# Sample attention of a two-layer decoder: the next batch's scores move between this batch's products

## The chip, the cores and the metric

The kernel runs on one core of a Trainium2 chip. The metric is the device time of one execution in microseconds (us). TensorE (PE) multiplies, VectorE (DVE) and ScalarE (ACT) work on what it leaves in PSUM, SyncE (SP) issues the loads from HBM.

## The reference, cut to what matters

Two layers are computed for 512 prompt tokens and for 8 sample batches of 4 tokens; the change lies in the native sparse attention (NSA) of the sample batches alone. Each batch has 4096 past positions in pages of 128, chosen by a page table.

```python
s_c = einsum('btkgd,bckd->bkgtc', qg, kc)            # compressed branch: 128 block means
p_c = masked_softmax(s_c, ...); o_c = p_c @ vc
imp = p_c summed over the heads of a group           # importance of each 64-key block
idx = top_k(score(imp), 16)                          # 16 blocks are selected
s_s = q @ selected keys;  o_s = softmax(s_s) @ selected values
s_w = q @ window keys;    o_w = softmax(s_w) @ window values
out = gate0 * o_c + gate1 * o_s + gate2 * o_w
```

## The kernel before, in words

The program runs in stages; each engine has its own instruction list, written out by hand, and waits on semaphores. `sample_attention_stage` works batch by batch (i = 0..7). It scores all 4096 past keys and adds a large negative number to the blocks that were not selected. The past is cut in 4 chunks c; a chunk is 512 columns of the tile `x` (`s_all` in rows), 4 pages for each of two halves of the past.

The steps of a batch, by the names that the text uses:

- **selection**: `select_scores` and `select_importance` on PE (L2890, L2902), `select_weights` (maximum, sum, division, L3080 to L3088) and `select_blocks` (top 16, L3094 to L3109) on DVE, `select` on ACT (L3044). The compressed weights lie in `pc`, which `turn(REST)` reads once more.
- **scores**: `score(i, c)` on PE (L2890) waits for the pages of chunk c; `mask_past` on DVE adds the block mask (L3130) and takes the chunk's maximum (L3136). `score_window` and `mask_window` do the same for the window and the new tokens.
- **the maximum over both halves**: L3139 on DVE, `swap_max` on PE (L2926), L3143 on DVE, which gives `neg_max`.
- **softening**: `soften` on ACT (L3052 the window, L3055 the chunks), all with the batch's `neg_max`.
- **products**: `turn(c)` on PE transposes a chunk (L2956), DVE or ACT copies it out (L3155, L3061), `multiply(c)`, called "out c", multiplies with the values (L2994). `REST` is the window, the compressed branch and the new tokens.
- **the end**: `fold_sums` on PE (L3002), `scales` and `combine` on DVE (L3164 to L3182), `end` on PE (L3008) and `place` on DVE (L3192).

Keys and values come through a ring of 11 slots (`PageRing`). A group is 4 pages of 256 KB, 8 groups make a batch, and a window of 1024 KB is loaded beside them: 9.44 MB for each batch. SP asks for group n when "out" of the chunk that held group n - 11 is done, and it takes the groups strictly in order. So of a batch's eight groups the first three can be asked for while the batch before it is still waiting for its softening, and the fourth (called +3) waits for "out 0" of the batch before:

```python
freed = n - RING_GROUPS
if freed >= 0:
    after(sp, pe_sum, f"out {freed % LOAD_GROUPS // 2}", freed // LOAD_GROUPS)
ring.load_pages(sp, n)
```

`x`, `neg_max` and the score banks (2 in PSUM) have one copy or two; a bank of scores is used again once its mask has been added.

Of the kernel before, what the change touches and what calls it, by code (L numbers as in the profile page):

```python
# [16 lines left out]
ALU = mybir.AluOpType  # L17
# [3 lines left out]
P = 128  # L21
# [22 lines left out]
SEL = 64  # L44
# [2769 lines left out]
def sample_attention_stage(nc, g, ring):  # L2814
# [4 lines left out]
    with Stage(nc, "satt") as st:  # L2819
        x = st.sb("s_all", [P, KEYS])  # L2820
        pc = [st.sb(f"pc{s}", [P, BLOCKS]) for s in range(2)]
        pT = st.sb("pT", [P, SLOTS_T, P])
# [15 lines left out]
        pe_select = st.line("pe_select", ["cmp scores", "importance"])  # L2838
        pe_score = st.line("pe_score", ["win scores"] + [f"scores {c}" for c in chunks] + ["swapped"])
        pe_sum = st.line("pe_sum", ["turn 0"] + [s for c in chunks for s in (f"turn {c + 1}", f"out {c}")]  # L2840
# [3 lines left out]
                                            "out a", "top b", "out b", "unselected"])  # L2844
        dve_score = st.line("dve_score", ["win masked", "win max"]
                            + [s for c in chunks for s in (f"masked {c}", f"max {c}")] + ["slc max", "max"])
        dve_sum = st.line("dve_sum", [f"turned {n}" for n in (0, 2, REST)]
                          + ["sum", "floor", "inverse", "scale", "slc", "win", "out"])
        dve_end = st.line("dve_end", ["placed"])
# [21 lines left out]
        with st.block() as block:  # L2871
# [14 lines left out]
            def _(pe):  # L2886
# [13 lines left out]
                def select_importance(i):  # L2900
                    after(pe, dve_select, "cmp p", i)
                    pe.matmul(ps_cmp[:, BLOCKS:2 * BLOCKS], g.const("group_sum"), pc[i % 2][:, :],  # L2902
                              start=True, stop=True).then_inc(*pe_select.done("importance"))
# [25 lines left out]
                def turn(n, i):  # L2929
                    if n == REST:  # L2930
# [7 lines left out]
                        pe.transpose(bank[:, 2 * P:3 * P], pc[i % 2][:, :], ident)  # L2938
                        small = g.const("ident", ROWS)[:, 0:ROWS]
# [71 lines left out]
                for i in range(2):  # L3011
                    select_scores(i)
                    select_importance(i)
                    if i == 0:
                        score_window(0)
                        for c in chunks:
                            score(0, c)
                        swap_max(0)
                for i in range(DEC_BATCH):
                    turn(0, i)  # L3020
                    for c in chunks:
                        turn(c + 1, i)
                        multiply(c, i)
                    multiply(REST, i)
                    fold_sums(i)
                    if i + 2 < DEC_BATCH:
                        select_scores(i + 2)
                        select_importance(i + 2)
                    if i + 1 < DEC_BATCH:
                        score_window(i + 1)  # L3030
                        for c in chunks:
                            score(i + 1, c)
                            if c == 0:
                                end(i)
                        swap_max(i + 1)
                    else:
                        end(i)

            @block.scalar
            def _(act):  # L3040
                def select(i):
                    after(act, dve_select, "cmp max", i)
                    after(act, pe_sum, f"turn {REST}", i - 2)
                    act.activation(pc[i % 2][:, :], ps_cmp[:, 0:BLOCKS], ACT.Exp, bias=cmp_max[:, 0:1],  # L3044
                                   accum_out=cmp_sum[:, 0:1]).then_inc(*act_select.done("cmp exp"))
# [30 lines left out]
            def _(dve):  # L3076
                def select_weights(i):
                    s = i % 2
                    after(dve, pe_select, "cmp scores", i)
# [44 lines left out]

                def mask_past(i):
                    after(dve, dve_select, "unselected", i)
                    per = 512 // SEL
                    for c in chunks:
                        after(dve, pe_score, f"scores {c}", i)
                        dve.tensor_tensor(  # L3130
                            x[:, columns(c)].rearrange("r (s k) -> r s k", k=SEL),
                            ps[c % 2][:, :].rearrange("r (s k) -> r s k", k=SEL),
                            unselected[i % 2][:, c * per:(c + 1) * per].unsqueeze(2).broadcast_to([P, per, SEL]),
                            ALU.add).then_inc(*dve_score.done(f"masked {c}"))
                        after(dve, dve_score, f"masked {c}", i)
                        dve.tensor_reduce(part_max[:, c:c + 1], x[:, softened(c)], AX_X, ALU.max, negate=True  # L3136
                                          ).then_inc(*dve_score.done(f"max {c}"))
# [20 lines left out]

                def scales(i):
                    after(dve, act_soften, f"exp {CHUNKS_KV - 1}", i)  # L3160
                    dve.tensor_reduce(both_sum[:, 0:1], part_sum[:, :], AX_X, ALU.add
                                      ).then_inc(*dve_sum.done("sum"))
                    after(dve, pe_sum, "folded", i)
                    dve.tensor_scalar(scale[:, :], whole_sum, 1e-30, None, ALU.max).then_inc(*dve_sum.done("floor"))  # L3164
# [32 lines left out]
                select_weights(0)  # L3197
                select_blocks(0)
                mask_window(0)
                mask_past(0)  # L3200
                select_weights(1)
                select_blocks(1)
                for i in range(DEC_BATCH):
                    turned(0, i)
                    turned(2, i)
                    turned(REST, i)
                    scales(i)
                    combine(i)
                    if i + 2 < DEC_BATCH:
                        select_weights(i + 2)  # L3210
                        select_blocks(i + 2)
                    if i + 1 < DEC_BATCH:
                        mask_window(i + 1)
                        mask_past(i + 1)
                    place(i)
# [181 lines left out]
```

## Time and profile before

| | us |
|---|---|
| median of 3 runs (lowest, highest) | 2037.99 (2037.88, 2048.09) |
| the profiled execution: its time, its span | 2041.63, 2039.4 |
| stage of the change, in the span | 1422.6 to 1645.2 |
| PE, DVE, ACT busy over the whole span | 1600.0, 795.7, 499.5 |

The span runs from the first to the last instruction; the stage of the change is 222.6 us of it. Busy shares of the whole span mix stages with different limits, so the rows below are taken from this stage alone. In a timeline row the numbers at the front are the start and the length, and the brackets at its end give the idle time of that engine ahead of the row and what ended it.

### The profile page before, as it was taken

The numbers are of one execution on the slowest core, as the hardware profiler recorded it, in microseconds if no ns is written. First come the engines' busy times: TensorE is split into PE (matmuls) and PEld (weight loads), VectorE is DVE, ScalarE is ACT, GpSimd is POOL, SyncE is SP. The second block draws the span as 40 slices with busy tenths as digits, with TensorE's granted clock in tenths as the row PEclk, the third lists the DMA queues.
The fourth block names the chain that finished last, engine by engine and source line by source line (L and its number), as shares of the span: only waits on it lengthen the run. The fifth ranks groups of instructions, "written<-read, shape, count | busy, mean of one in ns | idle before, by whom it ended". The sixth has DMA issues, their size and how long they took to land. (4 is left out here: it accounts for less than half of the span.)

```text
span 2039.4 us, 34809 instructions
## 1 busy us (share of the span) xinstructions
PE 1600.0 (78%) x12618; PEld 1161.3 (57%) x12618; DVE 795.7 (39%) x1832; ACT 499.5 (24%) x1254; POOL 183.7 (9%) x282
## 2 busy tenths in 40 slices
PE   4999987799969498876799778886766688498874
PEld 3888867577746254443688655653433366255443
DVE  1888653456422311112123337665545413211112
ACT  2111662133211111110200146775111111111110
POOL 0111002312010311110000000000000000311110
PEclk8999986888779699897699977998777789699997
DMA  3777855200048299995166530004799847299995
GB/s 130 247 252 249 265 204 206 85 5 5 4 167 339 67 386 424 423 424 198 65 216 216 165 128 1 2 2 150 284 348 354 289 165 316 85 423 424 423 417 177
DMA packets 130913, 445.12 MB, mean 218 GB/s; under 512 B 22033, under 2 KB 27666, under 8 KB 112722
## 3 DMA queue, kind: packets, MB, share of 16 engines
q1 hardware_dynamic: 114562, 423.08, 55.2%
q0 software_dynamic: 11008, 17.89, 2.4%
q10 hardware_dynamic: 5200, 2.23, 0.4%
q8 instruction: 92, 1.51, 0.3%
q14 instruction: 51, 0.42, 0.1%
HBM read 427.01 MB, written 44.42 MB: 231 GB/s over the span
## 5 line engine op out<-in xcount | busy, mean ns | idle before, releaser
L435 PE MATMUL proj_acc<-h_gdn,proj_w 128*128 128x272 f32 x1024 | 238.3, 395 | 14.3 <-DMA proj_w<-in_gdn_w 14.3
L435 PEld LDWEIGHTS proj_acc<-h_gdn,proj_w 128*128 128x128 f32 x1024 | 196.0, 192 | 55.5 <-DMA proj_w<-in_gdn_w 14.7
L1984 PE MATMUL moe_experts_bank_gu<-moe_weights_gu,mix 128*64 128x256 f32 x1024 | 133.8, 427 | 30.7 <-DMA moe_weights_gu<-in_w_gate_up 29.0
L2225 PE MATMUL nproj_acc<-nsa_h,nproj_w 128*128 128x272 f32 x640 | 147.7, 394 | 0.0
L2225 PEld LDWEIGHTS nproj_acc<-nsa_h,nproj_w 128*128 128x128 f32 x640 | 122.1, 191 | 25.3
L1984 PEld LDWEIGHTS moe_experts_bank_gu<-moe_weights_gu,mix 128*64 128x64 f32 x1024 | 88.8, 155 | 80.5 <-issue 53.4
L1984 PE MATMUL moe_experts_bank_gu<-moe_weights_gu,moe_experts_room 128*64 128x256 f32 x1024 | 120.5, 396 | 16.8 <-issue 16.8
L1738 PE MATMUL moe_front_acc<-mix,moe_front_wo 128*128 128x272 f32 x512 | 121.4, 401 | 15.3 <-DMA moe_front_wo<-in_gdn_wo 9.0
L1738 PEld LDWEIGHTS moe_front_acc<-mix,moe_front_wo 128*128 128x128 f32 x512 | 99.5, 195 | 36.9 <-DMA moe_front_wo<-in_gdn_wo 9.4
L1984 PEld LDWEIGHTS moe_experts_bank_gu<-moe_weights_gu,moe_experts_room 128*64 128x64 f32 x1024 | 86.1, 143 | 57.0 <-issue 28.8
L289 DVE TENSOR_REDUCE first_sums<-proj_raw 128x2560 f32 (+1 forms) x32 | 98.6, 3080 | 29.7 <-DMA proj_raw<-in_cmp_pool 29.7
L1691 POOL DMA_INDIRECT table<-moe_front_entry,moe_front_slot_of x20 | 19.2, 962 | 913.0 <-DVE moe_front_place L1634 794.3
L289 DVE TENSOR_REDUCE nsa_past_c<-nproj_raw 128x2048 f32 x20 | 45.7, 2286 | 125.7 <-DMA nproj_raw<-in_cmp_pool 125.7
L2629 ACT ACTIVATE patt_p<-patt_p,patt_neg_max 128x512 f32<-128x512 f32 (+3 forms) x128 | 70.3, 550 | 30.1 <-DVE patt_neg_max L2530 30.1
L2530 DVE CUSTOM_DVE_ANT_0 patt_p<-patt_scores,patt_mask 128x512 f32<-128x512 f32 (+3 forms) x128 | 55.2, 487 | 53.4 <-PE patt_scores L2461 53.4
L2474 PE MATMUL patt_turn<-consts,patt_p 128*128 128x128 f32 x320 | 51.2, 293 | 28.0 <-DVE patt_p L2551 25.4
L2064 DVE SCALAR_TENSOR_TENSOR mix<-moe_experts_bank_gu,moe_table,mix 128x128 f32<-128x128 f32 x32 | 11.2, 351 | 154.2 <-ACT mix L2029 154.2
L2005 PE MATMUL moe_experts_bank_y<-moe_weights_down,moe_experts_room 128*64 128x512 f32 x256 | 58.5, 598 | 13.1 <-ACT moe_experts_room L2034 13.1
L2005 PE MATMUL moe_experts_bank_y<-moe_weights_down,mix 128*64 128x512 f32 x256 | 58.5, 598 | 10.1 <-ACT mix L2034 10.1
L2474 PEld LDWEIGHTS patt_turn<-consts,patt_p 128*128 128x128 f32 x320 | 35.8, 144 | 43.8 <-DVE patt_p L2551 37.5
L1968 PE MATMUL moe_experts_bank_x<-consts,mix 128*128 128x128 f32 x144 | 21.4, 296 | 48.5 <-DMA mix<-h_rows,moe_experts_src 48.5
L2064 DVE SCALAR_TENSOR_TENSOR moe_experts_room<-moe_experts_bank_gu,moe_table,moe_experts_room 128x128 f32<-128x128 f32 x32 | 11.2, 351 | 123.0 <-ACT moe_experts_room L2029 123.0
(518 smaller groups left out, 2576.4 us busy)
## 6 DMA issues: line engine op xcount, KB each, us to landing
moe_weights_gu<-in_w_gate_up SPq DMA_DIRECT2D x64, 2048.0 KB, 31.8
moe_weights_down<-in_w_down SPq DMA_DIRECT2D x64, 1024.0 KB, 33.0
ring_rest_kv<-in_slc_pool SPq DMA_DIRECT2D x184, 256.0 KB, 4.9
proj_raw<-in_cmp_pool SPq DMA_DIRECT2D x176, 256.0 KB, 3.7
nproj_raw<-in_cmp_pool SPq DMA_DIRECT2D x80, 256.0 KB, 3.3
ring_kv_first<-in_slc_pool SPq DMA_DIRECT2D x72, 256.0 KB, 4.7
proj_w<-in_gdn_w SPq DMA_DIRECT2D x32, 512.0 KB, 4.3
nproj_w<-in_nsa_w SPq DMA_DIRECT2D x20, 512.0 KB, 3.6
```

The lines of the kernel that those rows point to most:

```text
L289: dve.tensor_reduce(self.out[:, bass.ds(at, per), :].rearrange("p g c -> p (g c)"), self.raw[s][:, 0:per, :].rearrange("p g (c t) -> p (g ...
L435: mm = pe.matmul(acc[s][:, a, 0:HALF], w[s][:, k, :], g.hT[:, k, a * HALF:(a + 1) * HALF], start=(k == 0), stop=(k == KT - 1))
L1691: pool.indirect_dma_start(out=flat, out_offset=bass.IndirectOffsetOnAxis(ap=slot_of[j][0:n, t:t + 1], axis=0), in_=entry[j][0:n, t, :], in ...
L1738: mm = pe.matmul(acc[m % 2][:, a, 0:HALF], wo[m % 2][:, k, :], src[:, k, a * HALF:(a + 1) * HALF], start=(k == 0), stop=(k == KT - 1))
L1968: mm = pe.transpose(x_bank[k // 4][:, (k % 4) * P:(k % 4 + 1) * P], ln.x[:, k * P:(k + 1) * P], ident)
L1984: mm = pe.matmul(gu_bank[m][H, 0:FF], ln.xT[:, k, H], w.gu[:, k, m * FF:(m + 1) * FF], start=(k == 0), stop=(k == KT - 1))
L2005: mm = pe.matmul(y_bank[a][H, :], ln.hT[:, at:at + SLOTS], w.down[:, m, a * 512:(a + 1) * 512], start=(m == 0), stop=(m == 1))
L2064: dve.scalar_tensor_tensor(out=ln.h[:, m * P:(m + 1) * P], in0=gu_bank[m][:, P:2 * P], scalar=weight.bitcast(F32), in1=ln.gate[:, m * P:(m ...
L2225: mm = pe.matmul(acc[s][:, a, 0:HALF], w[s][:, k, :], g.hT[:, k, a * HALF:(a + 1) * HALF], start=(k == 0), stop=(k == KT - 1))
L2474: mm = pe.transpose(turn[(4 * u + m) % TURN_BANKS][:, tile(b)], p[u % P_BUFFERS][:, s, a, tile(b)], ident)
L2530: dve.tensor_tensor_reduce(p[u % P_BUFFERS][:, s, a, 0:n], scores[m][:, 0:n], mask[:, SEQ - n:SEQ], -(HD ** -0.5), 1e30, ALU.add, ALU.min, ...
L2629: act.activation(part, part, ACT.Exp, scale=-1.0, bias=neg_max[u % 2][:, m:m + 1], accum_out=sums[u % 2][:, s, a:a + 1]).then_inc(*act_e.d ...
```

## The change

On PE, after "out 1" of batch i, the scores of batch i + 1 are issued a chunk at a time between the products of batch i: chunk 0 after out 1, chunk 1 after out 2, chunk 2 after out 3, then the window and chunk 3 after the rest products. The selection for batch i + 2 is spread over the middle of batch i, and `select_blocks(i + 1)` stands behind the first copy of batch i. The end of batch i (`fold_sums`, `scales`, `combine`, `end`, `place`) now stands behind the last scores and the maximum of batch i + 1. `pc` gets a third buffer, since the selection of i + 2 now writes it before batch i has read its own. What is loaded, its order, and what frees a slot stay as they were, and so does the arithmetic.

```diff
-        pc = [st.sb(f"pc{s}", [P, BLOCKS]) for s in range(2)]
+        pc = [st.sb(f"pc{s}", [P, BLOCKS]) for s in range(3)]
...
                 for i in range(2):
                     select_scores(i)
                     select_importance(i)
-                    if i == 0:
-                        score_window(0)
-                        for c in chunks:
-                            score(0, c)
-                        swap_max(0)
+                for c in chunks[:-1]:
+                    score(0, c)
+                score_window(0)
+                score(0, CHUNKS_KV - 1)
+                swap_max(0)
                 for i in range(DEC_BATCH):
+                    more = i + 1 < DEC_BATCH
                     turn(0, i)
                     for c in chunks:
                         turn(c + 1, i)
                         multiply(c, i)
+                        if more and c >= 1:
+                            score(i + 1, c - 1)
+                        if i + 2 < DEC_BATCH and c == 1:
+                            select_scores(i + 2)
+                        if i + 2 < DEC_BATCH and c == 3:
+                            select_importance(i + 2)
                     multiply(REST, i)
+                    if more:
+                        score_window(i + 1)
+                        score(i + 1, CHUNKS_KV - 1)
                     fold_sums(i)
-                    if i + 2 < DEC_BATCH:
-                        select_scores(i + 2)
-                        select_importance(i + 2)
-                    if i + 1 < DEC_BATCH:
-                        score_window(i + 1)
-                        for c in chunks:
-                            score(i + 1, c)
-                            if c == 0:
-                                end(i)
+                    if more:
                         swap_max(i + 1)
-                    else:
-                        end(i)
+                    end(i)
...
                 for i in range(DEC_BATCH):
+                    more = i + 1 < DEC_BATCH
                     turned(0, i)
+                    if more:
+                        select_blocks(i + 1)
                     turned(2, i)
+                    sum_parts(i)
+                    if more:
+                        mask_past(i + 1, 0)
+                        mask_past(i + 1, 1)
+                    if i + 2 < DEC_BATCH:
+                        select_weights(i + 2)
                     turned(REST, i)
+                    if more:
+                        mask_past(i + 1, 2)
+                        mask_window(i + 1)
+                        mask_past(i + 1, CHUNKS_KV - 1)
+                        whole_max(i + 1)
                     scales(i)
                     combine(i)
-                    if i + 2 < DEC_BATCH:
-                        select_weights(i + 2)
-                        select_blocks(i + 2)
-                    if i + 1 < DEC_BATCH:
-                        mask_window(i + 1)
-                        mask_past(i + 1)
                     place(i)
```

On DVE, `select_weights(1)` also moves ahead of the first masks of batch 0, and `select_blocks(1)` behind the first copy.

PE from the fold of batch 1 to the first product of batch 2, before (`satt_out` is the combined output of a batch, `satt_both_max` the maxima that are swapped):

```order
L3002 MATMUL satt_end<-satt_both_sum,nsa_consts 128x2
L2890 MATMUL satt_cmp<-nsa_past_c,nsa_qb 32x128 x4
L2902 MATMUL satt_cmp<-satt_pc,nsa_consts 128x128
L2890 MATMUL satt_new<-nsa_k_new,nsa_qb 32x64 x4
L2890 MATMUL satt_new<-ring_rest_win,nsa_qb 32x256 x4
L2890 MATMUL satt_scores<-ring_rest_kv,nsa_qb 32x512 x4
L3008 MATMUL satt_end<-nsa_consts,satt_out 128x64
...
L2926 MATMUL satt_new<-satt_both_max,consts 128x2
L2956 MATMUL satt_turn<-consts,satt_s_all 128x128 x8
L2994 MATMUL satt_out_acc<-ring_rest_kv,satt_pT 32x128 x16
```

The same place in the change, from the scores of the last chunk:

```order
L2891 MATMUL satt_scores<-ring_kv_first,nsa_qb 32x512 x4
L3003 MATMUL satt_end<-satt_both_sum,nsa_consts 128x2
L2927 MATMUL satt_new<-satt_both_max,consts 128x2
L3009 MATMUL satt_end<-nsa_consts,satt_out 128x64
L2957 MATMUL satt_turn<-consts,satt_s_all 128x128 x8
L2995 MATMUL satt_out_acc<-ring_rest_kv,satt_pT 32x128 x16
```

The selection and the earlier scores have left this place, and the end (L3008, now L3009) has moved from behind the first chunk's scores to between the swap and the first transposes.

DVE from the last chunk's maximum of batch i + 1 to its first copy, before:

```order
L3136 TENSOR_REDUCE satt_part_max<-satt_s_all 128x1
L3139 TENSOR_REDUCE satt_both_max<-satt_part_max 128x1
L3143 TENSOR_TENSOR satt_neg_max<-satt_both_max,satt_new 128x2
L3192 COPY mix<-satt_end 64x8x4 x2
L3155 COPY satt_pT<-satt_turn 128x512 x2
```

The same place on DVE in the change:

```order
L3137 TENSOR_REDUCE satt_part_max<-satt_s_all 128x1
L3142 TENSOR_REDUCE satt_both_max<-satt_part_max 128x1
L3146 TENSOR_TENSOR satt_neg_max<-satt_both_max,satt_new 128x2
L3169 TENSOR_SCALAR satt_scale<-satt_end 128x2
L3171 RECIPROCAL satt_scale<-satt_scale 128x2
L3173 TENSOR_TENSOR satt_scale<-satt_scale,nsa_row_gates 128x2
L3179 TENSOR_SCALAR satt_out<-satt_out_acc,satt_scale 128x128
L3182 SCALAR_TENSOR_TENSOR satt_out<-satt_end,satt_scale,satt_out 128x128
L3187 SCALAR_TENSOR_TENSOR satt_out<-satt_end,nsa_row_gates,satt_out 64x128
L3197 COPY mix<-satt_end 64x8x4 x2
L3158 COPY satt_pT<-satt_turn 128x512
```

The six instructions of `scales` and `combine` have come in behind `neg_max`.

## Rows read from the trace of the kernel before

**Rows 1.** Busy time by stretch: engines, PE's clock, DMA share, GB/s.

```profile
1422.00:1444.00 22.00, 13.99 (x122) 7.36 (x126) 13.14 (x44) 4.81 (x15) 0.00 (x0) 0.66 0.53 193
1498.00:1525.00 27.00, 17.52 (x237) 10.42 (x229) 13.18 (x40) 5.04 (x14) 0.00 (x0) 0.81 0.97 349
```

**Rows 2.** Waits, us in total, times, longest; first two within the stage.

```profile
PE satt_scores L2890 <- DMA ring_rest_kv<-in_slc_pool: 13.1, 5, 3.8
PE satt_scores L2890 <- DMA ring_kv_first<-in_slc_pool: 5.4, 2, 2.8
...
SPq L2781 <- PE satt_out_acc L2994: 48.5, 8, 12.0
```

**Rows 3.** Timeline, one loop, from the last scores to the next last scores.

```profile
1515.84 1.06 PE L2890 MATMUL satt_scores<-ring_rest_kv,nsa_qb 128*32 128x512 f32 x8 [3.14 <-DMA ring_rest_kv<-in_slc_pool]
...
1519.35 0.16 DVE L3143 TENSOR_TENSOR satt_neg_max<-satt_both_max,satt_new 128x2 f32<-128x2 f32 x1 [0.75 <-PE satt_new L2926]
...
1520.92 1.97 PE L2956 MATMUL satt_turn<-consts,satt_s_all 128*128 128x128 f32 x8 [1.68 <-ACT satt_s_all L3055]
...
1522.08 0.69 DVE L3155 COPY satt_pT<-satt_turn 128x512 f32<-128x512 f32 x1 [2.27 <-PE satt_turn L2956]
...
1525.13 1.92 SPq L2786 DMA_DIRECT2D ring_kv_first<-in_slc_pool  x4
...
1543.35 1.07 PE L2890 MATMUL satt_scores<-ring_rest_kv,nsa_qb 128*32 128x512 f32 x8 [3.22 <-DMA ring_rest_kv<-in_slc_pool]
```

**Rows 4.** Timeline of SP ahead of its wait in the same loop.

```profile
1517.93 0.42 SPq L2791 DMA_DIRECT2D ring_rest_win<-in_win  x1
```

**Rows 5.** Busy time by stretch of 2 us, columns as in rows 1.

```profile
1520.00:1522.00 2.00, 1.07 (x5) 1.08 (x6) 0.00 (x0) 2.00 (x7) 0.00 (x0) 0.50 1.06 390
...
1524.00:1526.00 2.00, 2.00 (x52) 1.51 (x44) 0.69 (x1) 0.00 (x0) 0.00 (x0) 0.93 0.48 188
...
1528.00:1530.00 2.00, 2.00 (x57) 1.54 (x55) 0.80 (x3) 0.00 (x0) 0.00 (x0) 1.00 0.78 243
...
1624.00:1626.00 2.00, 0.97 (x8) 0.23 (x8) 0.00 (x0) 0.00 (x0) 0.00 (x0) 0.50 0.06 22
```

**Rows 6.** Timeline, scales, combine and end of a batch, at two places.

```profile
1510.22 0.49 PEld L3008 LDWEIGHTS satt_end<-nsa_consts,satt_out 128*128 128x128 f32 x2 [1.66 <-issue]
...
1510.78 0.16 PEld L2890 LDWEIGHTS satt_scores<-ring_rest_kv,nsa_qb 128*32 128x32 f32 x8
...
1612.67 0.16 DVE L3164 TENSOR_SCALAR satt_scale<-satt_end 128x2 f32<-128x2 f32 x1 [1.75 <-PE satt_end L3002]
...
1614.11 0.34 DVE L3182 SCALAR_TENSOR_TENSOR satt_out<-satt_end,nsa_row_gates,satt_out 64x128 f32<-64x128 f32 x1
...
1614.50 0.30 PEld L3008 LDWEIGHTS satt_end<-nsa_consts,satt_out 128*128 128x128 f32 x2 [1.24 <-DVE satt_out L3182]
```

**Rows 7.** Timeline of the head: first scores, selections of batches 0 and 1, out 0.

```profile
1426.38 0.20 PEld L2890 LDWEIGHTS satt_scores<-ring_kv_first,nsa_qb 128*32 128x32 f32 x4 [0.23 <-issue]
...
1427.60 0.36 DVE L3109 TENSOR_SCALAR satt_unselected<-satt_score 64x32 f32<-64x32 f32 x2
...
1435.40 0.29 DVE L3080 TENSOR_REDUCE satt_cmp_max<-satt_cmp 128x1 f32<-128x128 f32 x1 [0.16 <-PE satt_cmp L2890]
...
1436.95 0.50 PEld L2902 LDWEIGHTS satt_cmp<-satt_pc,nsa_consts 128*128 128x128 f32 x2 [1.88 <-DVE satt_pc L3088]
...
1440.68 1.48 PEld L2994 LDWEIGHTS satt_out_acc<-ring_kv_first,satt_pT 128*32 128x32 f32 x32 [1.63 <-DVE satt_pT L3155]
```

**Rows 8.** Timeline of the last loop: products at either clock, last scores.

```profile
1604.21 1.94 PE L2994 MATMUL satt_out_acc<-ring_rest_kv,satt_pT 128*32 128x128 f32 x32
...
1606.67 13.79 SPq L2786 DMA_DIRECT2D ring_rest_kv<-in_slc_pool  x20
...
1608.31 1.08 PE L2994 MATMUL satt_out_acc<-ring_rest_kv,satt_pT 128*32 128x128 f32 x32
...
1625.03 1.94 PE L2890 MATMUL satt_scores<-ring_rest_kv,nsa_qb 128*32 128x512 f32 x8 [3.48 <-issue]
```

More of the change, by code:

```diff
@@ L2838, in sample_attention_stage @@
         pe_select = st.line("pe_select", ["cmp scores", "importance"])
-        pe_score = st.line("pe_score", ["win scores"] + [f"scores {c}" for c in chunks] + ["swapped"])
+        pe_score = st.line("pe_score", [f"scores {c}" for c in chunks[:-1]]
+                           + ["win scores", f"scores {CHUNKS_KV - 1}", "swapped"])
         pe_sum = st.line("pe_sum", ["turn 0"] + [s for c in chunks for s in (f"turn {c + 1}", f"out {c}")]
@@ L2844, in sample_attention_stage @@
                                             "out a", "top b", "out b", "unselected"])
[L2845 to L2848, printed above, removed]
+        dve_score = st.line("dve_score", [s for c in chunks[:-1] for s in (f"masked {c}", f"max {c}")]
+                            + ["win masked", "win max", f"masked {CHUNKS_KV - 1}", f"max {CHUNKS_KV - 1}",
+                               "slc max", "max"])
+        dve_sum = st.line("dve_sum", ["turned 0", "turned 2", "sum", f"turned {REST}", "floor", "inverse", "scale", "slc", "win", "out"])
         dve_end = st.line("dve_end", ["placed"])
@@ L2937, in turn @@
                             pe.transpose(bank[:, m * P:(m + 1) * P], x[:, at:at + P], ident)
-                        pe.transpose(bank[:, 2 * P:3 * P], pc[i % 2][:, :], ident)
+                        pe.transpose(bank[:, 2 * P:3 * P], pc[i % 3][:, :], ident)
                         small = g.const("ident", ROWS)[:, 0:ROWS]
@@ L3042, in select @@
                     after(act, dve_select, "cmp max", i)
-                    after(act, pe_sum, f"turn {REST}", i - 2)
-                    act.activation(pc[i % 2][:, :], ps_cmp[:, 0:BLOCKS], ACT.Exp, bias=cmp_max[:, 0:1],
+                    after(act, pe_sum, f"turn {REST}", i - 3)
+                    act.activation(pc[i % 3][:, :], ps_cmp[:, 0:BLOCKS], ACT.Exp, bias=cmp_max[:, 0:1],
                                    accum_out=cmp_sum[:, 0:1]).then_inc(*act_select.done("cmp exp"))
@@ L3077, in select_weights @@
                 def select_weights(i):
-                    s = i % 2
+                    s = i % 3
                     after(dve, pe_select, "cmp scores", i)
@@ L3123, in mask_window, with mask_past, whole_max @@
                                       ).then_inc(*dve_score.done("win max"))
-                def mask_past(i):
+                def mask_past(i, c):
                     after(dve, dve_select, "unselected", i)
                     per = 512 // SEL
[L3128 to L3137, printed above, removed]
+                    after(dve, pe_score, f"scores {c}", i)
+                    dve.tensor_tensor(
+                        x[:, columns(c)].rearrange("r (s k) -> r s k", k=SEL),
+                        ps[c % 2][:, :].rearrange("r (s k) -> r s k", k=SEL),
+                        unselected[i % 2][:, c * per:(c + 1) * per].unsqueeze(2).broadcast_to([P, per, SEL]),
+                        ALU.add).then_inc(*dve_score.done(f"masked {c}"))
+                    after(dve, dve_score, f"masked {c}", i)
+                    dve.tensor_reduce(part_max[:, c:c + 1], x[:, softened(c)], AX_X, ALU.max, negate=True
+                                      ).then_inc(*dve_score.done(f"max {c}"))
+                def whole_max(i):
                     after(dve, dve_score, f"max {CHUNKS_KV - 1}", i)
@@ L3157, in turned, with sum_parts @@
                     ins.then_inc(*dve_sum.done(f"turned {n}"))
-                def scales(i):
+                def sum_parts(i):
                     after(dve, act_soften, f"exp {CHUNKS_KV - 1}", i)
@@ L3162, in scales @@
                                       ).then_inc(*dve_sum.done("sum"))
+                def scales(i):
                     after(dve, pe_sum, "folded", i)
@@ L3198, in _ @@
                 select_blocks(0)
+                select_weights(1)
+                for c in chunks[:-1]:
+                    mask_past(0, c)
                 mask_window(0)
-                mask_past(0)
-                select_weights(1)
-                select_blocks(1)
+                mask_past(0, CHUNKS_KV - 1)
+                whole_max(0)
                 for i in range(DEC_BATCH):
+                    more = i + 1 < DEC_BATCH
                     turned(0, i)
+                    if more:
+                        select_blocks(i + 1)
                     turned(2, i)
-                    turned(REST, i)
+                    sum_parts(i)
[4 more added lines that the diff above has]
+                        select_weights(i + 2)
+                    turned(REST, i)
+                    if more:
[3 more added lines that the diff above has]
+                        whole_max(i + 1)
                     scales(i)
                     combine(i)
-                    if i + 2 < DEC_BATCH:
-                        select_weights(i + 2)
-                        select_blocks(i + 2)
-                    if i + 1 < DEC_BATCH:
-                        mask_window(i + 1)
-                        mask_past(i + 1)
                     place(i)
```

2 lines of the change are left out of this document (1 added, 1 removed).

## The prediction

> **What bounds the kernel now.** I went first to the stretches of the sample attention. Eight batches take about 27 us each, and in such a stretch PE is busy for two thirds, DVE for half, and the DMA engines for 0.97 of the time, at 349 GB/s [rows 1]. That looks like a bound by DMA, so I asked the waits: within the stage PE waited for loads seven times, once for each batch from 1 to 7, 18.5 us in all, and SP waited eight times for the products that free a slot of the ring, 48.5 us [rows 2]. Each waits for the other: a loop. The timeline shows its links. The last scores of a batch begin when their pages land (1515.84); mask, maximum, swap, softening, transpose and copy follow, out 0 frees the first slots, and SP goes on at 1525.13. I call this part **A**, 9.29 us. Then five groups have to be asked for and to land before the next last scores at 1543.35: part **B**, 18.22 us [rows 3]. A + B = 27.51 us, the period. The last loop repeats it: SP at 1606.67, last scores at 1625.03, B = 18.36 [rows 8].
>
> During A, SP can ask for three groups and the window only; it had done that by 1518.35 [rows 4] and then stood. The loads in flight ran on at 390 GB/s and dried up: 188 GB/s at 1524 to 1526, still 243 at 1528 to 1530 [rows 5]. So the DMA engines are busy in most of the loop, but the loop is closed by the path of A, not by what the engines could move. Only what lies in A or B counts. The selection and the first three chunks' scores do not: in this loop PE was through with them 3.14 us before the pages came [rows 3].
>
> **The change, part by part.**
>
> *Selection and early scores move between the products.* They leave a stretch of PE and DVE that ended in a wait for pages. What hid them was B, and B stays: the same loads, order and releases. I count 0; the end of that stretch comes earlier, the landing does not. Without that cover the most to be had would be the wait itself, 18.5 us [rows 2], if the loads came sooner too; that is a rival below.
>
> *The end of batch i moves into A.* PE takes its instructions in order, and `end` now stands ahead of the first transposes of the next batch; it waits for `scales` and `combine`, which DVE now runs behind `neg_max`. Queued behind it on PE are turn 0, turn 1 and out 0; SP waits for out 0. Before, turn 0 began 1.41 us after `neg_max` was written (1519.51 to 1520.92), the time of two softenings on ACT [rows 3]. Now: scales and combine take 1.78 us (1612.67 to 1614.45), PE starts 0.05 later, and from the end's weight load to the next load it was 0.56 us at half clock (1510.22 to 1510.78), 0.30 or a little more at full clock [rows 6]. With 0.03 ahead of it that is 2.2 to 2.4 us instead of 1.41: 0.8 to 1.0 us more, and I take 1.0, since the granted clock in this part of A is 0.50 [rows 5]. The softenings run beside it. Each of the seven batches 1 to 7 has this once: **+7.0 us** (5.6 to 7.0). `place` waits for `end`, but it is done before turn 0 is, so the copy behind it loses nothing. The fold and the maximum ahead of it have their inputs early.
>
> *The clock at the last scores.* Now PE works through its batch up to the last scores and only then waits. After the change it meets three waits on pages in a batch: chunk 1 needs group +3, which SP asks for only after out 0, chunk 2 needs +5, chunk 3 needs +7. By 390 GB/s a group of 1.05 MB takes 2.69 us; counted back from the landing of +7 at B = 18.2 us they land at about 7.4, 12.8 and 18.2 us after out 0. Between them PE has only a product chunk or two (1.08 us each at full clock [rows 8]). Where waits already lay like that, in batch 7, the last scores ran at half clock: 1.94 us at a granted clock of 0.50, against 1.06 [rows 3, 5, 8]. The other six may fall to that: 6 x 0.87 = **+5.2 us** (0 to 5.2). The Trainium skill says the same of such a pattern ("TensorE: Matmul & The Clock Gate", section on HAM oscillation): short bursts of products between waits on DMA put the clock back to half in every round; the trace agrees in the one batch that waits so. By that rule the whole 5.2 is due; by the six fast rows alone nothing is.
>
> *Does PE still get to the last scores in time?* After the landing of +5 at 12.8 come chunk 2's scores (1.06 to 1.94), the importance (0.50 and a gap of 0.2 [rows 7]), the rest products (taken as one out chunk, 1.08 to 1.94 [rows 8]) and the window's scores (half a chunk's columns in two parts, taken as one chunk at full clock, 1.1): 3.9 to 5.7 us, so 16.7 to 18.5 against 18.2. At full clock there is room, at half clock it is late by 0.3 us. I take 0, at most 7 x 0.3 = 2.1.
>
> *The head.* Batch 0 has no loop ahead of it; its out 0 at 1440.68 [rows 7] starts the loads again, so a shift here shifts everything. Its scores now wait for the selection of batch 1 too, since `select_importance(1)` stands ahead of them on PE. `select_weights(1)` can begin when `select_blocks(0)` ends (1427.60 + 0.36 = 1427.96), takes 1.55 us to the importance (1435.40 to 1436.95), whose load and the gap behind it take 0.7 (0.50 and 0.2): first scores at 1430.2 instead of 1426.38 [rows 7]. The last chunk's scores begin after three chunks (1.06 to 1.94 each) and the window (1.1): 1434.5 to 1437.1. From there to the end of the copy it was 6.93 us (1515.84 to 1522.77 [rows 3]), perhaps 0.9 more at half clock: out 0 at 1441.4 to 1444.9, 0.7 to 4.2 us late. What it wins back, the selection of batch 1 that stood ahead of the first copy, is in this already. The granted clock of this stretch was 0.66 [rows 1], so I take the upper part: **+3.0 us**.
>
> The third `pc` buffer, the sum that stands earlier on DVE, and `select_blocks` behind the first copy cost nothing: they stand behind the first copy, so out 0 does not wait for them, and out 1, which does wait for the second copy, is needed by SP only after two more groups (2 x 2.69 us).
>
> **Sum:** 7.0 + 5.2 + 3.0 = 15.2 us. Bounds: 5.6 + 0 + 0.7 = 6.3 and 7.0 + 5.2 + 2.1 + 4.2 = 18.5. Against the profiled execution (2041.6) that is 2056.8 us. The median of the runs before is 3.6 us below that execution, so the forecast for the median is 2038.0 + 15.2 = **2053.2 us**; this case's own range is 2044 to 2057.
>
> **The rivals.** A measurement of this kernel can tell about 0.5% (10 us) from no change.
>
> *Faster: the ring stops running dry.* If out 0 came soon enough that the engines stay filled, a batch would take its bytes at the steady rate: 9.44 MB at 390 GB/s = 24.2 us, 3.3 less than 27.5, seven times: -23, with the head's 3 about -20, **2018 us**. It decides at the place where SP waits (1518.35 to 1525.13 [rows 3, 4]): A would have to shrink by the 3 us that the dry spell costs, from 9.3 to about 6. For it speaks that DMA is the engine with the largest share and that PE, DVE and the selection get much room; against it, that no step of A is taken out and one is put in. The Trainium skill ("DMA: Bandwidth & Descriptors", section "Where 436 GB/s comes from") puts the HBM side of a core at about 358 GB/s; 9.44 MB would then take an estimated 26.4 us, and this rival would win only some 5 us, 2033 us. The trace disagrees, 390 GB/s over 2 us [rows 5]. Chance 0.13.
>
> *About the same: PE keeps its full clock through A.* The work spread over the batch could keep the clock up. Then out 0 takes 1.08 instead of 1.94 us [rows 8] each time: A gets 0.9 shorter, the end costs 0.8, the last scores nothing. 7 x (0.8 - 0.9) + 3.0 = about 2: **2040 us**, and up to 2047 where it holds in part, or where the clock term is missing and the head is at its low bound. Against it: A still holds the gaps for mask, maximum and softening in which the clock fell to 0.50 [rows 5]. Chance 0.27.
>
> *Slower than forecast: PE becomes late* at half clock through the batch, or the end costs more: 2058 to 2070 us. Chance 0.08.
>
> My forecast keeps 0.52. The range leaves out the faster rival and the far end of the slower one: 2035 to 2061. Faster by over 0.5%: 0.13. Within 0.5%, from the second rival and the low end of my own range (2044 to 2048, a tenth of the chance): 0.32. Slower: 0.55.
>
> **What would show it.** In the profile after: SP still waits for out products about eight times, nearer 8 us each than 6; the period between last scores is 28.5 to 29.5 us; PE's transposes of chunk 0 wait for `satt_out` through `end` (L3009), not for ACT; PE waits for pages about three times in a batch instead of once, with a granted clock below 0.81 in these stretches; the importance no longer waits for `satt_pc`; out 0 of batch 0 comes some 3 us later. I am wrong if the period falls under 27 us (the loop is not what I take it for), if turn 0 still begins 1.4 us after `neg_max`, or if the DMA rate no longer dips below 300 GB/s once in a batch.

## The result and the profile after

The changed kernel took 2053.97 us (median of 14 runs, 2050.00 to 2056.45) against 2042.62 us for the kernel before on the same chip (median of 14, 2037.88 to 2048.09): a ratio of 1.0053, 95% interval 1.0042 to 1.0064, so 11.35 us slower. (Of the runs in the next section one execution, 2731.62 us in e10, is left out of the ratio; the other five of that kernel lie between 2019.54 and 2026.28.) The profiled execution has a span of 2054.3 us, 14.9 longer than before; 3.9 of that lie ahead of the changed stage, which begins at 1426.56 instead of 1422.64, in code that the change does not touch. That start differs from one profiled execution to the next: in the six kernels with 11 slots that were profiled for this text it lies between 1422.64 and 1430.71, with the same code ahead of it. So these 3.9 us are not put down to the change.

The stage by stretches (columns as in [rows 1]); the last four rows of 2 us answer to [rows 5]:

```profile
1476.00:1504.00 28.00, 19.73 (x235) 10.88 (x234) 12.50 (x37) 2.93 (x9) 0.00 (x0) 0.68 0.88 318
1509.00:1536.00 27.00, 19.34 (x230) 11.03 (x233) 12.84 (x37) 5.13 (x14) 0.00 (x0) 0.73 0.98 348
1536.00:1564.00 28.00, 19.87 (x222) 11.08 (x215) 11.66 (x34) 4.17 (x12) 0.00 (x0) 0.68 0.93 328
...
1534.00:1536.00 2.00, 2.00 (x28) 1.59 (x31) 1.83 (x7) 0.81 (x3) 0.00 (x0) 0.50 0.86 352
1536.00:1538.00 2.00, 2.00 (x28) 1.25 (x24) 0.88 (x6) 0.00 (x0) 0.00 (x0) 0.50 0.09 35
1538.00:1540.00 2.00, 2.00 (x48) 1.33 (x40) 0.65 (x2) 0.00 (x0) 0.00 (x0) 0.85 0.86 272
1549.00:1551.00 2.00, 0.63 (x4) 0.23 (x8) 0.00 (x0) 0.00 (x0) 0.00 (x0) 0.50 0.99 341
```

PE's granted clock fell from 0.81 to about 0.7 and with it PE looks busier, with the same work. The dry spell of the ring is deeper: 35 GB/s in the 2 us in which SP goes on (1537.23), where the same place in the loop before had 188 [rows 5].

The waits (us in total, times, longest), the first three within the stage; they answer to [rows 2]:

```profile
PE satt_scores L2891 <- issue: 36.2, 19, 3.8
...
PEld satt_end L3009 <- DVE satt_out L3187: 16.5, 8, 2.1
...
PEld satt_cmp L2903 <- issue: 9.1, 6, 1.7
...
SPq L2781 <- PE satt_out_acc L2995: 59.9, 10, 14.3
```

PE now stops nineteen times ahead of scores in the loops, not eight: the seven of [rows 2], and the one ahead of the last scores of batch 7, which the profile before put under "issue" [rows 8]. Here the profile names no releaser either. That all nineteen are waits for pages is read from the landings that the trace records: each of these scores begins 0.09 us after the last of its pages has landed, and the mask that empties its bank had ended 8.2 us earlier or more. The importance (L2903) waits for `satt_pc` nowhere in the loops any more, though it still has idle time that no row explains. SP waits 11.4 us longer in all, in ten waits instead of eight.

One loop, from last scores to last scores, for [rows 3] and [rows 4]:

```profile
1527.17 1.06 PE L2891 MATMUL satt_scores<-ring_rest_kv,nsa_qb 128*32 128x512 f32 x8 [0.82 <-issue]
...
1529.87 0.42 SPq L2791 DMA_DIRECT2D ring_rest_win<-in_win  x1
...
1530.55 0.16 DVE L3146 TENSOR_TENSOR satt_neg_max<-satt_both_max,satt_new 128x2 f32<-128x2 f32 x1 [0.55 <-PE satt_new L2927]
...
1532.45 0.50 PEld L3009 LDWEIGHTS satt_end<-nsa_consts,satt_out 128*128 128x128 f32 x2 [2.09 <-DVE satt_out L3187]
1532.72 1.72 PEld L2957 LDWEIGHTS satt_turn<-consts,satt_s_all 128*128 128x128 f32 x8
...
1537.23 1.88 SPq L2786 DMA_DIRECT2D ring_kv_first<-in_slc_pool  x4
...
1543.88 1.07 PE L2891 MATMUL satt_scores<-ring_kv_first,nsa_qb 128*32 128x512 f32 x8 [2.01 <-issue]
...
1550.37 1.93 PE L2891 MATMUL satt_scores<-ring_rest_kv,nsa_qb 128*32 128x512 f32 x8 [2.80 <-issue]
...
1556.44 1.93 PE L2891 MATMUL satt_scores<-ring_rest_kv,nsa_qb 128*32 128x512 f32 x8
```

The chain of A can be followed link by link: last scores, `neg_max`, the wait of `end` for `satt_out`, the transposes, SP at 1537.23. A took 10.06 us here instead of 9.29, and SP stood for 6.94 us (from 1530.29) instead of 6.78. The scores of chunks 1 and 2 come after waits, and those of chunk 2 run at half clock (1.93 against 1.07), as do the last scores, which here waited for nothing: their pages had landed at 1555.51, 0.93 us before PE came to them, so PE itself was late.

The head, for [rows 7]:

```profile
1426.56 0.23 PEld L2891 LDWEIGHTS satt_cmp<-nsa_past_c,nsa_qb 128*32 128x32 f32 x8 [1.66 <-issue]
...
1433.46 0.50 PEld L2903 LDWEIGHTS satt_cmp<-satt_pc,nsa_consts 128*128 128x128 f32 x2 [3.15 <-DVE satt_pc L3090]
...
1434.18 0.20 PEld L2891 LDWEIGHTS satt_scores<-ring_kv_first,nsa_qb 128*32 128x32 f32 x8 [0.23 <-issue]
...
1447.44 1.48 PEld L2995 LDWEIGHTS satt_out_acc<-ring_kv_first,satt_pT 128*32 128x32 f32 x32 [0.33 <-DVE satt_pT L3158]
```

The first scores now stand behind the importance of batch 1. From the weight load of the stage's first product to out 0 it was 20.88 us, before 18.04 (1422.64 to 1440.68 [rows 7]).

So the stage can be laid out in three pieces, each from trace starts:

| | before | after | |
|---|---|---|---|
| head: first product to out 0 of batch 0 | 18.04 | 20.88 | +2.84 |
| seven loops: out 0 of batch 0 to out 0 of batch 7 | 192.20 (1440.68 to 1632.88) | 200.40 (1447.44 to 1647.84) | +8.20 |
| tail: out 0 of batch 7 to the last `place` | 11.97 (to 1644.85) | 11.40 (to 1659.24) | -0.57 |

The rows of these starts that are not shown above, two from before and one from after:

```profile
1422.64 0.23 PEld L2890 LDWEIGHTS satt_cmp<-nsa_past_c,nsa_qb 128*32 128x32 f32 x8 [1.66 <-issue]
...
1632.88 1.48 PEld L2994 LDWEIGHTS satt_out_acc<-ring_kv_first,satt_pT 128*32 128x32 f32 x32 [0.33 <-DVE satt_pT L3155]
...
1647.84 1.48 PEld L2995 LDWEIGHTS satt_out_acc<-ring_kv_first,satt_pT 128*32 128x32 f32 x32 [0.33 <-DVE satt_pT L3158]
```

Together +10.5 us, which is nearly all of the 11.35. The tail says little: where nothing in it was changed it was 11.97 (before), 10.62 (e4) and 10.86 (e5).

### The profile page after: what moved, and what is told of

It reads as the page before. It is cut to its first block and busy times, and to the rows that moved or that the text cites. A ratio compares the mean times of both kernels' runs of the same rounds, so it can differ in the third digit from the quotient of the medians.

```text
span 2054.3 us, 34832 instructions
## 1 busy us (share of the span) xinstructions
PE 1619.6 (79%) x12618; PEld 1173.0 (57%) x12618; DVE 796.9 (39%) x1832; ACT 499.9 (24%) x1254; POOL 183.4 (9%) x282
## 5 line engine op out<-in xcount | busy, mean ns | idle before, releaser
L1984 PE MATMUL moe_experts_bank_gu<-moe_weights_gu,mix 128*64 128x256 f32 x1024 | 135.0, 430 | 30.4 <-DMA moe_weights_gu<-in_w_gate_up 28.7
L2225 PEld LDWEIGHTS nproj_acc<-nsa_h,nproj_w 128*128 128x128 f32 x640 | 122.2, 191 | 25.4
L2474 PE MATMUL patt_turn<-consts,patt_p 128*128 128x128 f32 x320 | 51.2, 293 | 28.0 <-DVE patt_p L2551 25.4
L2891 PE MATMUL satt_scores<-ring_rest_kv,nsa_qb 128*32 128x512 f32 x184 | 37.1, 810 | 31.1 <-issue 31.1
```

The source lines that it names most:

```text
L1984: mm = pe.matmul(gu_bank[m][H, 0:FF], ln.xT[:, k, H], w.gu[:, k, m * FF:(m + 1) * FF], start=(k == 0), stop=(k == KT - 1))
L2225: mm = pe.matmul(acc[s][:, a, 0:HALF], w[s][:, k, :], g.hT[:, k, a * HALF:(a + 1) * HALF], start=(k == 0), stop=(k == KT - 1))
L2474: mm = pe.transpose(turn[(4 * u + m) % TURN_BANKS][:, tile(b)], p[u % P_BUFFERS][:, s, a, tile(b)], ident)
L2891: mm = pe.matmul(out_[quarter(half, pair), :], g.qb[:, pair, i, :], rhs(half, pair), start=True, stop=True)
```

## The experiments

Ratios are to the kernel before, run on the same chip, with the 95% interval. "Loops" is the second piece of the table above, in the one profiled execution.

**e1: before, with only the end moved into A.** On PE `end(i)` moves behind `swap_max(i + 1)`, on DVE `scales` and `combine` behind the next masks; the sum stays early as in the change. Selection and scores stay where they were.

```diff
                         for c in chunks:
                             score(i + 1, c)
-                            if c == 0:
-                                end(i)
                         swap_max(i + 1)
-                    else:
-                        end(i)
+                    end(i)
```

> The kernel before, with only one part of the change: scales, combine and end of a batch stand behind the maximum of the next batch (the sum stays early, so that nothing deadlocks). Loop theory: A, the path from the last scores to out 0, gets longer by what the changed kernel shows, about 0.75 us (neg_max to out 0: 4.2 instead of 3.5 us), seven times: +5.3 us, ratio 1.002 to 1.004; SP's stop grows from 6.5 to some 7.3 us a batch. Rival (the place of the end costs nothing, the change lost its time by PE's clock alone): ratio 1.000, 3.5 us from neg_max to out 0.

Measured: 2051.89 us, 1.0038 [1.0022, 1.0055]; loops 205.86. The end alone gives a slowdown of 4.5 to 11 us, with out 0 4.22 us behind `neg_max`, as in the changed kernel:

```profile
1523.59 1.94 PE L2890 MATMUL satt_scores<-ring_rest_kv,nsa_qb 128*32 128x512 f32 x8 [4.39 <-DMA ring_rest_kv<-in_slc_pool]
...
1527.97 0.16 DVE L3140 TENSOR_TENSOR satt_neg_max<-satt_both_max,satt_new 128x2 f32<-128x2 f32 x1 [0.75 <-PE satt_new L2926]
...
1529.87 0.50 PEld L3008 LDWEIGHTS satt_end<-nsa_consts,satt_out 128*128 128x128 f32 x2 [2.09 <-DVE satt_out L3181]
...
1530.35 1.92 PE L2956 MATMUL satt_turn<-consts,satt_s_all 128*128 128x128 f32 x8
```

Out 0 follows at 1532.20. Here PE waits for pages ahead of the last scores of every batch, and longer than before (4.39 us against 3.14), and all seven last scores ran at half clock, against one of seven before. So the end brought the clock term with it in this execution: over the seven loops the stretch from last scores to `neg_max` is 5.2 us longer than before (30.7 against 25.4) and the stretch from `neg_max` to out 0 another 5.2. The reading is that a later out 0 makes the next pages later, and that the longer wait ends at the lower clock. SP's stop grew to a mean of 8.9 us, more than the 7.3 that was expected. The profiled execution was a long one, 2057.17 us against a median of 2051.89, so its loops overstate the step.

**e2: the changed kernel, with the end taken out of A again.** The fold goes directly behind the rest products, `scales` and `combine` behind the mask of chunk 2, `end` between the last scores and the swap.

```diff
                     multiply(REST, i)
+                    fold_sums(i)
                     if more:
                         score_window(i + 1)
                         score(i + 1, CHUNKS_KV - 1)
-                    fold_sums(i)
+                    end(i)
                     if more:
                         swap_max(i + 1)
-                    end(i)
```

> The changed kernel, with scales and combine ahead of the window's masks and end ahead of the swap, so that nothing of the old batch stands between neg_max and the first transposes. Loop theory: 5.3 us come back, ratio to the kernel before 1.002 to 1.004 instead of 1.005; neg_max to turn 0 is 1.6 us again. DVE may be late for the last mask by up to 1 us a batch, which would eat the gain. Rival (clock alone): ratio stays at 1.005.

Measured: 2049.87 us, 1.0034 [1.0017, 1.0051]; loops 198.81. The transposes follow `neg_max` by 1.58 us again:

```profile
1646.93 0.16 DVE L3146 TENSOR_TENSOR satt_neg_max<-satt_both_max,satt_new 128x2 f32<-128x2 f32 x1 [0.55 <-PE satt_new L2927]
...
1648.51 1.97 PE L2957 MATMUL satt_turn<-consts,satt_s_all 128*128 128x128 f32 x8 [1.68 <-ACT satt_s_all L3057]
```

The gain over the change is 0.0019, about 4 us; the intervals of the two overlap, so by time alone this is not settled, but the link in the trace is back at its old length in every batch (3.47 us from `neg_max` to out 0, where the change has 4.15 to 4.23 and before had 3.45 to 3.48). Those 5.2 us did not come back whole: the loops are only 1.6 us shorter than in the change, since the stretch from last scores to `neg_max`, where DVE now has `combine` to do as well, grew by 1.5 (28.6 against 27.0) and the stretch from out 0 to the next last scores by 2.1.

**e3: e2, with the head as before.** The selection of batch 1 stands behind the maximum of batch 0 again, on PE and on DVE.

```diff
-                for i in range(2):
-                    select_scores(i)
-                    select_importance(i)
+                select_scores(0)
+                select_importance(0)
                 for c in chunks[:-1]:
                     score(0, c)
                 score_window(0)
                 score(0, CHUNKS_KV - 1)
                 swap_max(0)
+                select_scores(1)
+                select_importance(1)
```

> As the run before, and the selection of batch 1 stands behind the first batch's maximum again, as in the kernel before. Loop theory: another 2.8 us back, ratio 1.000 to 1.003; what is left is PE's clock and lateness at the last scores, and the interleaved selection and scores by themselves win nothing. Rival (interleaving wins by itself, the end and the head hid it): ratio under 0.999, period under 27.2 us.

Measured: 2046.61 us, 1.0008 [0.9994, 1.0023]; loops 196.22. What is left of the change is its main idea, scores and selection spread between the products, and by time it is worth nothing here: no gain, no loss that can be told. In the one trace this is a balance: the loops are 4.0 us longer than before, the head 1.3 shorter (16.74) and the tail 1.5 shorter, which is about what a tail differs by where nothing in it was changed. The step from e2 is 0.0026, some 5 us with about 4 either way; in the traces the head gives 4.15 of it (20.89 in e2). The head is shorter than before because `select_blocks(1)` stays behind the first copy, as in the change: from `neg_max` to out 0 of batch 0 it is 4.29 us, before it was 5.59. The last wait of A ends as before:

```profile
1524.25 0.16 DVE L3147 TENSOR_TENSOR satt_neg_max<-satt_both_max,satt_new 128x2 f32<-128x2 f32 x1 [0.55 <-PE satt_new L2927]
...
1525.82 1.97 PE L2957 MATMUL satt_turn<-consts,satt_s_all 128*128 128x128 f32 x8 [1.68 <-ACT satt_s_all L3058]
...
1529.91 1.36 SPq L2786 DMA_DIRECT2D ring_kv_first<-in_slc_pool  x3
```

**e4 and e5: before, with a ring of 10 and of 12 slots.** This asks whether the loop is closed by A and the ring at all. Nothing else is changed.

```diff
-RING_GROUPS = 11
+RING_GROUPS = 10     # e4; 12 in e5
```

> The kernel before with a ring of 10 slots instead of 11. Loop theory: one group more has to be asked for after out 0, B grows by 2.4 to 2.7 us, seven times: +17 to +19 us, ratio 1.008 to 1.009, and SP's stop grows by about 2.5 us a batch. Rival (the rate of the DMA engines or the work of PE sets the period, the ring is no bound): ratio within 1.002.

> The kernel before with a ring of 12 slots. Loop theory: four groups and the window can be asked for during A, so one group less stands in B: 2.5 us a batch less until the engines' own rate (24.2 us a batch) or PE (2.8 to 3.2 us of wait left at the last scores) ends it: -15 to -18 us, ratio 0.991 to 0.993; the DMA rate no longer dips to 190 GB/s once a batch. Rival (the engines, busy 0.97 of the time, set the period): within 0.2% of before.

Measured: 10 slots 2064.04 us, 1.0111 [1.0083, 1.0138], loops 218.54; 12 slots 2026.64 us, 0.9929 [0.9914, 0.9943], loops 180.61. With one slot fewer SP stops 10.4 us in a loop and the DMA engines run empty (e4, timeline of SP: the window's request and the next one after the stop):

```profile
1526.58 0.42 SPq L2791 DMA_DIRECT2D ring_rest_win<-in_win  x1
...
1537.36 2.73 SPq L2786 DMA_DIRECT2D ring_rest_kv<-in_slc_pool  x5
```

Stretches of 2 us in that stop, columns as in [rows 1]:

```profile
1534.00:1536.00 2.00, 2.00 (x29) 1.58 (x31) 0.69 (x1) 1.61 (x5) 0.00 (x0) 0.50 0.05 16
1536.00:1538.00 2.00, 2.00 (x40) 1.43 (x36) 0.38 (x1) 0.00 (x0) 0.00 (x0) 0.72 0.00 0
```

With one more its stops are 4.1 to 7.3 us (5.9 to 6.9 before), and the rate over a whole loop rises (e5, two loops, columns as in [rows 1]; a packet is counted where it starts, so a share can pass 1). Its lowest stretches of 2 us in these loops carry 281 and 243 GB/s.

```profile
1496.00:1522.00 26.00, 18.92 (x237) 11.23 (x241) 13.29 (x40) 5.04 (x14) 0.00 (x0) 0.76 1.03 370
1522.00:1548.00 26.00, 18.65 (x254) 10.72 (x247) 13.21 (x40) 5.04 (x14) 0.00 (x0) 0.83 1.00 358
```

Its wait for out products, over the whole span (48.5 us before [rows 2]):

```profile
SPq L2781 <- PE satt_out_acc L2994: 39.6, 7, 9.7
```

One slot is worth 26.3 us of loops downward and 11.6 upward, by time 20.0 and 14.6. Ten slots cost more than the 17 to 19 us that were expected: SP's stop grew by 4.2 us, not 2.5, and all seven last scores ran at half clock, as in e1. So the loop is what the prediction took it for, and the engines, busy for 0.97 of the time [rows 1], had room left.

**e6 and e7: the change, and e3, with 12 slots.** If spreading the work pays only where pages come sooner, it should show here.

```diff
-RING_GROUPS = 11
+RING_GROUPS = 12     # e6: in the changed kernel; e7: in e3
```

> The changed kernel with a ring of 12 slots. Loop theory: the same group is taken out of B, but the engines' rate is a floor for both, and the interleaving now has room to count, since pages no longer come last: ratio to the kernel before 0.992 to 0.997, that is still up to 9 us above the run with 12 slots on the kernel before (head 3, end 0.75 a batch where it is not hidden). If the interleaved scores are worth something once the ring is deeper, it comes out at or below that run.

> The interleaved scores and selection alone (end and head as in the kernel before, by the edits of the two runs above), with 12 slots. Loop theory: same as the kernel before with 12 slots, 0.990 to 0.993, or lower by up to 1 us a batch if PE's own work had become the bound there. If the interleaving costs by PE's clock at the last scores, it is above that run by up to 5 us.

Measured: e6 2032.05 us, 0.9958 [0.9942, 0.9975]; e7 2026.76 us, 0.9928 [0.9913, 0.9943]. Beside e5 (0.9929) the change as it stands costs 5.4 us, and spreading alone again gives nothing. In the traces 2.85 of the 5.4 are the head (20.89 against 18.04) and only 1.2 the loops (181.85 against 180.61), although out 0 again comes 4.15 to 4.22 us behind `neg_max`; what hides the rest of the end there is not shown.

**e8: before, with the window's softening later.** A shorter A is the other way to feed the ring. ACT softens the window (0.5 us) ahead of chunk 0; it is put behind chunk 1.

```diff
-                        if c == 0:
+                        if c == 2:
                             act.activation(x[:, SLC_END:KEYS], x[:, SLC_END:KEYS], ACT.Exp, bias=neg_max[:, 1:2],
```

> The kernel before, with the window's softening on ACT behind chunk 1's instead of ahead of chunk 0's. Loop theory: turn 0 waits for one softening less, A is 0.6 us shorter, eight times (the head too): -4 to -5 us, ratio 0.9975 to 0.998; neg_max to out 0 is 2.8 to 2.9 us instead of 3.5. Rival (A is no part of the bound): 1.000.

Measured: 2040.92 us, 0.9992 [0.9978, 1.0006]; loops 189.96, 2.24 less. By time it cannot be told from no change, and 0.9975 to 0.998, which was expected, is at the edge of the interval. In the trace the transposes start 1.06 us behind `neg_max`, not 1.57:

```profile
1521.75 0.16 DVE L3143 TENSOR_TENSOR satt_neg_max<-satt_both_max,satt_new 128x2 f32<-128x2 f32 x1 [0.75 <-PE satt_new L2926]
...
1522.81 1.97 PE L2956 MATMUL satt_turn<-consts,satt_s_all 128*128 128x128 f32 x8 [1.17 <-ACT satt_s_all L3055]
```

0.5 us in each of seven loops would be 3.5; 2.2 came back, with two last scores at half clock instead of one. The head, which was to get shorter too, did not: 18.04 us, as before.

**e9 and e10: what beats both kernels.** e9 is before with 12 slots and the later window softening; e10 is e7 with the later window softening (the two edits shown above).

> The kernel before with 12 slots and the window's softening behind chunk 1's. Loop theory: if the ring is still the bound at 12 slots (a batch takes 25.8 us there, above the 24.2 of the engines' rate), the 0.5 us that this edit takes out of A count again: 0.9925 or a little lower, down to 0.991. If PE and DVE set the period by now, the gain is the same 0.5 us a batch, since A is on their path too; only if the engines' rate is the floor does it stay at 0.993.

> Interleaved scores and selection, end and head as before, 12 slots, and the window's softening behind chunk 1's. Same as the run beside it if interleaving is worth nothing, 0.991 to 0.993; below it by up to 5 us if the work of PE and DVE outside A was what held the other one.

Measured: e9 2025.13 us, 0.9914 [0.9893, 0.9935], loops 176.95; e10 2023.88 us, 0.9902 [0.9879, 0.9924], loops 175.68. Both beat both kernels; which of the two is better is open. The loops of e9 are 3.7 us shorter than those of e5 (180.61), about seven times the 0.5 us that A lost: there the shorter A counts in full.

## Why the prediction was right

The sign and the place were right: slower, through A, the clock and the head. The single number (2053.2 against 2053.97) is closer than the working deserves: the sum was about 4 us too large (15.2 against 11.35), and the median of three that it was added to (2038.0) lay 4.6 below the later one of fourteen. The two errors cancel, and that is luck.

| step | forecast | measured in the trace |
|---|---|---|
| selection and early scores, off the path | 0 | 0 as far as time can tell (e3: 1.0008; e7 as e5) |
| the end of batch i in A | +7.0 | +5.2 |
| the clock at the last scores | +5.2 | about +1.6 |
| PE late | 0 (up to 2.1) | about +1.4 |
| the head | +3.0 | +2.84 |
| the tail | not counted | -0.57, less than it differs by unchanged |

*The end in A.* From `neg_max` to out 0 it was 3.45 to 3.48 us before; the change has 4.15 for batch 1 and 4.23 for the six others: 0.69 + 6 x 0.76 = 5.2. The forecast had 0.8 to 1.0 a batch and took 1.0. It put turn 0 at 2.2 to 2.4 us after `neg_max` was written (1530.71); turn 0's weight load began 2.01 us after it and its products 2.22, where both had 1.41 before. What was too large is the distance from the end's weight load to the next load, taken as 0.56 at half clock [rows 6]. It was 0.27, at a granted clock of 0.50: turn 0's load begins at 1532.72, while the end's own load (0.50 long) is still going on. The load behind `end` in [rows 6] was that of a score product; that a transpose would follow as late was an assumption. That the end costs time is shown by e1, and by the link that returns to its old length in e2; its size by time alone only within e1's interval.

*The clock.* The forecast took all six full-speed last scores down to half clock. From last scores to `neg_max` the full-clock value was 3.48 to 3.51 before; after, three of seven were long (batches 1, 2 and 4: 4.45, 4.81, 4.26) and the four others, with the swap sooner, 3.38. That is 27.0 us against 25.4 over the seven, the latter with one long one (batch 7, 4.38). The granted clock of the stretches did fall as forecast (below 0.81 everywhere), but most of that slow work ran off the path: the scores of chunk 2 ran at half clock in six batches of seven. The Trainium skill ("TensorE: Matmul & The Clock Gate", section on HAM oscillation) has the clock return to half in every round of short work between DMA waits; the traces agree for the last scores of three batches of seven here and of all seven in e1 and e4, and not for the rest. What decides between the rounds was not tried.

*PE late.* In two loops the last scores waited for nothing (1498.00, 1556.44). Their pages had landed 0.74 and 0.93 us earlier, where scores that wait begin 0.09 after the landing: PE was late by 1.5 us in all. It fits what is left of the loops: from out 0 to the next last scores they take 143.9 us in all against 142.5, with these two 1.1 longer each and the other five 0.8 shorter together. The prediction had lateness at up to 0.3 a batch at half clock; it came in two batches, by more.

*The head* was right in size, by out 0, and it is the best shown of the terms: it took 18.04 us in all six profiled kernels that have the head of before (before, e1, e4, e5, e8, e9), 20.88 or 20.89 with the selection of batch 1 ahead of the scores (the change, e2, e6), and 16.74 with that selection moved back (e3, e7, e10). So the selection on the path costs 4.15, and `select_blocks(1)` behind the first copy wins 1.30 back; the prediction had both in its one term.

*A reading.* The prediction has PE wait for loads seven times, 18.5 us in all. It was eight and 22.0: batch 7 waited ahead of its last scores too, 3.48 us, which the profile calls "issue" [rows 8] though the trace has these pages landing 0.09 us before. Only the bound of the faster rival rests on it.

*What would show it.* SP's stops grew from 5.9 to 6.9 us to a mean of 8.0, the period between last scores is 28.7 us ((1640.23 - 1468.16) / 6), the transposes wait through `end`, PE waits for pages two to three times a batch: each about as forecast.

*The rivals.* The faster one, that the ring stops running dry, is a real mechanism, but nothing in this change reaches it; one slot more goes most of the way (e5, whose lowest 2 us carry 243 GB/s), and with A shorter too a loop comes down to 25.1 us (e10, 175.68 / 7), near the 24.2 that the prediction had put as its end. The second, that PE keeps its full clock through A, fell: the granted clock around out 0 is 0.50 as before.

Open: why some last scores ran at half clock and others not, and with it how much of the 11.35 us is the clock's.

## What to carry to other kernels

Where a ring of buffers is refilled by a late step of the same work, price a reordering by what stands between the last landing and the first release: whatever leaves the rest of the loop is worth nothing, whatever enters this path is paid once a round. A DMA share near 1 does not show that DMA is the bound; ask who waits for whom, and try one slot more before reordering an engine's list. Look at the head by itself: work that is harmless in a loop delays the first release of all when it stands ahead of it.

## What the hardware showed that was not expected

The DMA engines carried 349 GB/s at a busy share of 0.97 [rows 1] and still 370 GB/s over 26 us, at a share of 1.03, with one slot more: the share alone did not tell the room that was left. The figure that the prediction weighed, about 358 GB/s on the HBM side of a core (the Trainium skill, "DMA: Bandwidth & Descriptors", section "Where 436 GB/s comes from"), is passed in that loop and met in the next one (358).

A wait for pages that grew by about 1 us (3.14 to 4.39 us, e1) came with the doubling of the products behind it (1.06 to 1.94 us), so a later page cost more than its own delay: 0.87 us more from last scores to `neg_max` (4.38 against 3.51). It happened in all seven batches of e1 and of e4, in one before, and in three of the changed kernel, in two of them with no wait directly ahead of the last scores.
